# A decoder layer on one core: w_up too in Strassen products, 256 tokens wide, with sums of its blocks on GpSimd

## The chip, the cores and the metric

The kernel runs on one core of one Trainium2 chip. Its engines are TensorE (PE, matmuls and transposes), VectorE (DVE), ScalarE (ACT), GpSimd (POOL) and SyncE (SP, which only issues DMAs here). The metric is the device time of one execution in microseconds (us).

## What is computed

One hybrid decoder layer on 512 tokens of width 1024, all in float32:

```python
    hn = rms_norm(h, mix_pre_g)                     # w_in: q, k, v, u, gv
    ... MoBA attention beside chunked gMLP gating, both through w_o
    h = h + rms_norm(mixed @ w_o, mix_post_g)
    hn = rms_norm(h, mlp_pre_g)
    ff = square(relu(hn @ w_up))                    # (512, 1024) @ (1024, 4096)
    h = h + rms_norm(ff @ w_down, mlp_post_g)       # (512, 4096) @ (4096, 1024)
    gate = sigmoid(h @ w_ple_gate + b_ple_gate)
    h = h + rms_norm((p @ w_ple) * gate, ple_post_g)
```

The change is in the two products of the channel MLP, `w_up` and `w_down`, and in what stands around them.

## The kernel before

**Products in three matmuls.** Every float32 operand x is split in two parts of the faster type float32r: `x_hi` (ACT copies x, which rounds it) and `x_lo = x - x_hi` (DVE). A product is hi * hi + hi * lo + lo * hi, three matmuls into one PSUM bank (`product`, called on lines 1816 to 1821 of the profile). So each block of a weight or of activations costs one ACT and one DVE operation before PE may use it.

**The MLP in 8 steps.** A step is 512 of the 4096 hidden features. `up_tile(step, j)`, j from 0 to 3, makes 128 features by 512 tokens: 8 slices of the contraction by 3 matmuls, 24 matmuls of 512 columns. Its weights come as slabs of 128 x 512 through the buffer `raw` in SBUF, are multiplied by the gain `mlp_pre` in the split, and stay in a ring of 12 slots of `w_hi` and `w_lo`. ACT applies ReLU and square (`relu`, `f_square`) and leaves `f[step % 2]`, 4 tiles of 128 features by 512 tokens.

**w_down in Strassen products.** f and the step's 512 rows of `w_down` are each seen as 2 x 2 blocks (256 tokens by 256 features, 256 features by 512 columns). Seven products (`down_product(n)`, n = 7 * step + i, 12 matmuls of 512 columns) replace eight. Sums of f's blocks are made by DVE (`sum_e`, `sum_s2`, `sum_s3`, `sum_s4`). Sums of weight blocks are made by DMAs that add in SBUF, issued by POOL (`add_x`, `add_o`, lines 1674 and 1680), each behind the split of what the buffer held before. `t_split_hi` and `t_split_lo` split the weights (ring of 3), `a_split_hi` and `a_split_lo` the activations (ring of 4). `add_product` adds each filled product to `acc` in SBUF. PE's order for a step is product n, tile 0 of the next step, n+1, n+2, tile 1, n+3, tile 2, n+4, n+5, tile 3, n+6. The last step is done without Strassen, in 8 `down_tile`s of 12 matmuls.

**The order is written by hand.** Each engine has one queue, in program order: what waits at its head holds up all that is behind it. SP loads weights by its own list (`up_pair`, `x_raw`, `o_raw`), each entry behind the semaphore that frees its buffer.

**Around the MLP.** Before it, hn is turned by PE in 8 transposes (`turn_hn`), and ACT and DVE split the result from PSUM (`hn_turn_hi`, `hn_turn_lo`); `p @ w_ple` is computed and later spilled to DRAM (`ple_spill`), to make room for `acc`. After it, `add_mlp(t)` normalises `acc` and adds it to h, `turn_h2` transposes h, and `gate_tile` multiplies it by `w_ple_gate`. In the kernel before, h stays in SBUF all the time, and half of the gate's weights are split during the last steps.

Of the kernel before, what the change touches and what calls it, by code (L numbers as in the profile page):

```python
# [32 lines left out]
F32 = mybir.dt.float32  # L33
# [6 lines left out]
P = 128  # L40
# [29 lines left out]
SLAB_GATE = SLAB_UP + STEPS * KD  # L70
PAIRS_OF_SLABS = (SLAB_GATE + HALVES * KD) // 2
FIRST_PAIRS = KD // 2
UP_SLOTS = 12
# [15 lines left out]
T_RING, A_RING = 3, 4  # L89


def pair_in_stream(pair):

    first_up, first_gate = SLAB_UP // 2, SLAB_GATE // 2
    if pair < first_up:
        return pair
    if pair < first_gate:
        step, i = divmod(pair - first_up, KD // 2)
        return first_up + step // 2 * 16 + step % 2 * 4 + i
    return first_up + CHUNKS * 16 + pair - first_gate  # L100
# [31 lines left out]
def units_heads(unit):  # L132

    return [(s, pair, j) for s in range(2) for j, pair in enumerate(UNITS[unit][1])]

# [86 lines left out]
def hymba_layer(nc, x, xT, pT, weights, columns, rope, ws, rows, out):  # L222
# [6 lines left out]
    with ExitStack() as ctx:  # L229
# [44 lines left out]
        gain_post = place("gain_post", [P, D])  # L274
        at_work = top[0]
        work = place("work", [P, 2, W])
        at_junk = top[0]
# [27 lines left out]
        ple = place("ple", [P, TT, D], at=at_area)  # L305
# [10 lines left out]
        at_a = [at_area + 24 * KIB, at_area + 28 * KIB, at_area + 32 * KIB, at_junk]  # L316
# [3 lines left out]
        raw_x = [place(f"raw_x{i}", [P, 2, W], at=at_w_hi + 24 * KIB + 4 * KIB * i) for i in range(2)]  # L320
        raw_o = [place(f"raw_o{i}", [P, 2, W], at=at_w_lo + 24 * KIB + 4 * KIB * i) for i in range(2)]
# [79 lines left out]
        x_added, o_added = sem("x_added"), sem("o_added")  # L401
        t_hi_done, t_lo_done, a_hi_done, a_lo_done = (sem("t_hi_done"), sem("t_lo_done"),
# [14 lines left out]
        def ring(slab):  # L417
# [5 lines left out]
            i = slab - SLAB_GATE  # L423
            if i < KD:
                return (slab - SLAB_UP) % UP_SLOTS
            return UP_SLOTS + i - KD if i < KD + 4 else i - UP_SLOTS

        def gain_of(slab):
# [5 lines left out]
            if SLAB_UP <= slab < SLAB_GATE:  # L434
                return mlp_pre((slab - SLAB_UP) % KD)
# [8 lines left out]
        def raw_place(slab):  # L444
            if slab < KD:
                return first_raw[slab // 4][:, slab % 4, :]
            return raw[:, slab % 4, :]
# [22 lines left out]
        def last_weights(i):  # L470
# [4 lines left out]
            if i < 2:  # L475
                slot = (FIRST_LAST + i) % T_RING
                return source[:], t_hi[slot][:], t_lo[slot][:]
            return source[:], w_hi[:, 2 * i - 4:2 * i - 2, :], w_lo[:, 2 * i - 4:2 * i - 2, :]
# [1797 lines left out]
```

## Time and profile before

| | before |
|---|---|
| median of 3 runs (lowest to highest) | 599.71 us (599.58 to 599.74) |
| the profiled execution's own time | 599.75 us |
| its span in the profile | 598.0 us |
| PE, DVE, ACT, POOL busy | 99%, 65%, 52%, 14% |
| moved by DMA | 82.90 MB, 139 GB/s in the mean |

The span is what the hardware profiler recorded; the time of the execution is a little longer. Matmuls are pipelined: a matmul of 512 columns is drawn as 0.39 us long, and the next one starts before it ends. What counts is the distance from start to start.

### The profile page before, as it was taken

The page shows a single profiled execution, that of the slowest core. Times are in us where ns is not written, and L with a number is a line of the kernel's source. Part 1 is how long each engine was busy: PE and PEld are TensorE (multiplying, and loading weights), DVE is VectorE, ACT ScalarE, POOL GpSimd, SP SyncE. Part 2 cuts the span into 40 slices and gives each one's busy share as a digit, 9 for nine tenths or more (in the row PEclk, how much of TensorE's full clock was granted, in tenths as well). Part 3 has the DMA queues.
Part 4 walks back from the last instruction along what each step waited for, and adds up shares of the span by engine and source line. Part 5 has one row for each costly group of instructions (what it writes and reads, how often), then busy time and mean ns, then how long its engine had stood idle before and what let it go on. Part 6 is the DMA issues. An engine that isn't in the chain of part 4 may idle for free.

```text
span 598.0 us, 7772 instructions
## 1 busy us (share of the span) xinstructions
PE 589.8 (99%) x2920; PEld 491.2 (82%) x2920; DVE 389.1 (65%) x577; ACT 311.3 (52%) x541; POOL 82.4 (14%) x151
## 2 busy tenths in 40 slices
PE   9999999999999999999999999999999999999995
PEld 7888888888788888888888888888888888888885
DVE  5655544478765963956846938657667578569655
ACT  6845544666555745644634735545446355634422
POOL 0165333000101210001001001010010010001011
PEclk9999999999999999999999999999999999999999
DMA  8845332113101389646826647547377366234011
GB/s 274 311 152 176 114 105 71 67 41 99 42 2 36 107 231 312 181 154 126 252 63 159 210 106 154 198 88 195 141 147 223 87 149 224 85 134 184 0 72 71
DMA packets 24517, 82.90 MB, mean 139 GB/s; under 512 B 2848, under 2 KB 4256, under 8 KB 23968
## 3 DMA queue, kind: packets, MB, share of 16 engines
q1 hardware_dynamic: 18576, 59.78, 28.6%
q0 software_dynamic: 4032, 14.68, 14.5%
q10 hardware_dynamic: 1872, 7.95, 3.8%
q8 instruction: 23, 0.38, 0.2%
q14 instruction: 14, 0.11, 0.1%
HBM read 78.20 MB, written 4.19 MB: 138 GB/s over the span
## 4 chain that ended last, share of the span: by engine, by line
PE 97%; DVE 2%; ACT 0%; issue 0%; POOL 0%; DVEq 0%; ACTq 0%
PE psum L1816 30%; PE psum L1820 30%; PE psum L1821 30%; PE psum L1871 2%; PE psum L2003 1%; PE psum L1983 1%; PE psum L1925 1%; PE psum L1885 1%; DVE w_lo L508 0%; DVE stat L631 0%; PE psum L1908 0%; DVE h L1007 0%; PE psum L1933 0%; ACT probs L1218 0%; DVE h L713 0%
## 5 line engine op out<-in xcount | busy, mean ns | idle before, releaser
L508 DVE SCALAR_TENSOR_TENSOR w_lo<-raw,cols,w_hi 128x512 fp32r<-128x512 f32 x112 | 82.9, 784 | 43.7 <-ACT w_hi L1076 43.7
L1816 PE MATMUL psum<-actT_hi,w_hi 128*128 128x512 f32 x256 | 99.6, 389 | 0.0
L1820 PE MATMUL psum<-actT_lo,w_hi 128*128 128x512 f32 x256 | 99.6, 389 | 0.0
L1821 PE MATMUL psum<-actT_hi,w_lo 128*128 128x512 f32 x256 | 99.6, 389 | 0.0
L1076 ACT ACTIVATE w_hi<-raw,cols 128x512 fp32r<-128x512 f32 x112 | 74.2, 714 | 43.7 <-PE psum L1816 22.2
L1816 PE MATMUL psum<-w_hi,actT_hi 128*128 128x512 f32 (+1 forms) x230 | 89.5, 389 | 0.0
L1821 PE MATMUL psum<-w_hi,actT_lo 128*128 128x512 f32 (+1 forms) x230 | 88.0, 383 | 0.0
L1820 PE MATMUL psum<-w_lo,actT_hi 128*128 128x512 f32 (+1 forms) x230 | 87.8, 382 | 0.0
L1816 PE MATMUL psum<-t_hi,a_hi 128*128 128x512 f32 x212 | 82.6, 389 | 0.0
L1821 PE MATMUL psum<-t_hi,a_lo 128*128 128x512 f32 x212 | 82.5, 389 | 0.0
L1820 PE MATMUL psum<-t_lo,a_hi 128*128 128x512 f32 x212 | 82.5, 389 | 0.0
L837 DVE TENSOR_TENSOR t_lo<-raw_x,t_hi 128x1024 fp32r<-128x1024 f32 x28 | 34.2, 1223 | 52.7 <-ACT t_hi L1382 52.6
L1816 PEld LDWEIGHTS psum<-actT_hi,w_hi 128*128 128x128 f32 x256 | 48.1, 188 | 10.1
L1821 PEld LDWEIGHTS psum<-actT_hi,w_lo 128*128 128x128 f32 x256 | 48.0, 188 | 10.0
L1820 PEld LDWEIGHTS psum<-actT_lo,w_hi 128*128 128x128 f32 x256 | 48.0, 188 | 9.9
L1674 POOL DMA_DIRECT2D raw_x<-weights_dram x21 | 18.5, 883 | 258.2 <-DVE t_lo L837 258.2
L1821 PEld LDWEIGHTS psum<-w_hi,actT_lo 128*128 128x128 f32 x230 | 43.2, 188 | 8.5
L1816 PEld LDWEIGHTS psum<-w_hi,actT_hi 128*128 128x128 f32 x230 | 43.3, 188 | 8.2
L1820 PEld LDWEIGHTS psum<-w_lo,actT_hi 128*128 128x128 f32 x230 | 43.3, 188 | 8.0
L896 DVE TENSOR_TENSOR acc<-acc,psum 128x512 f32<-128x512 f32 x76 | 49.0, 682 | 1.1 <-PE psum L1821 1.1
L1821 PEld LDWEIGHTS psum<-t_hi,a_lo 128*128 128x128 f32 x212 | 39.8, 188 | 8.3
L1816 PEld LDWEIGHTS psum<-t_hi,a_hi 128*128 128x128 f32 x212 | 39.8, 188 | 8.3
(187 smaller groups left out, 903.9 us busy)
## 6 DMA issues: line engine op xcount, KB each, us to landing
raw<-weights_dram SPq DMA_DIRECT2D x66, 512.0 KB, 3.7
raw_o<-weights_dram SPq DMA_DIRECT2D x23, 512.0 KB, 3.5
raw_x<-weights_dram POOLq DMA_DIRECT2D x21, 512.0 KB, 5.5
raw_x<-weights_dram SPq DMA_DIRECT2D x9, 512.0 KB, 5.2
raw_o<-weights_dram POOLq DMA_DIRECT2D x7, 512.0 KB, 9.1
h<-x_dram ACTq DMA_DIRECT2D x4, 512.0 KB, 5.0
ple_spill<-ple ACTq DMA_DIRECT2D x1, 2048.0 KB, 10.1
out_dram<-h SPq DMA_DIRECT2D x7, 256.0 KB, 2.0
```

The lines of the kernel that those rows point to most:

```text
L508: nc.vector.scalar_tensor_tensor(out=w_lo[:, place_at, :], in0=source, scalar=gain, in1=high, op0=ALU.mult, op1=ALU.subtract).then_inc(sla ...
L837: nc.vector.tensor_tensor(t_lo[n % T_RING][:], t_source(n), t_hi[n % T_RING][:].bitcast(F32), ALU.subtract).then_inc(t_lo_done, 1)
L896: nc.vector.tensor_tensor(part, part, bank, how).then_inc(product_added, 1)
L1076: nc.scalar.activation(w_hi[:, place_at, :], source, ACT.Copy, scale=gain).then_inc(slab_hi, 1)
L1674: nc.gpsimd.dma_start(raw_x[step % 2][:], weights[down_in_stream(step, rows, half)], accum_op=ALU.add).then_inc(x_added, 16)
L1816: begin = nc.tensor.matmul(out, a_hi, b_hi, start=first, stop=False, skip_group_check=read_between)
L1820: nc.tensor.matmul(out, a_hi, b_lo, start=False, stop=False, skip_group_check=read_between)
L1821: return nc.tensor.matmul(out, a_lo, b_hi, start=False, stop=last, skip_group_check=read_between)
L1871: mm = nc.tensor.transpose(psum[:, banks[name], j * P:(j + 1) * P], source[:, j * P:(j + 1) * P], ident[:])
L1885: mm = nc.tensor.matmul(out, wsT[:, g, :], gv[:, :, g * GD:(g + 1) * GD], start=True, stop=True)
L1925: nc.tensor.matmul(psum[:, BANK_O, 0:P], warm[:], warm[:], start=True, stop=True)
L1983: mm = nc.tensor.transpose(psum[:, bank + s, k * P:(k + 1) * P], probs[:, place_in_group(unit), s, k * P:(k + 1) * P], ident[:])
```

## The change

`w_up` of steps 1 to 7 is computed in seven Strassen products as well. The 1024 rows of the contraction are two halves of 512, the step's 512 features two of 256, and the tokens two halves of 256. A product is 24 matmuls of 256 columns: 2 tiles of features by 4 slices of a contraction half by 3, with 256 tokens as the moving operand. Four sums of x blocks are made once (POOL, `sum_x`, split by ACT and DVE). Four sums of weight blocks are made per step by POOL (`sum_blocks`) in the raw buffers. Two PSUM banks hold the products; ACT copies partial results out (`copy_c`), and DVE adds or subtracts (`c_sum`), so that the four blocks C_11, C_22, C_12, C_21 of f appear one after the other. The gain `mlp_pre` is now applied to hn, not to the weights. Step 0 keeps full products.

For room, h is written to DRAM (`h_spill`) before the MLP and read again after it; `raw_x` and `raw_o` lie where h was. The gain of the MLP's norm is loaded late, and the ring of activations has 3 slots.

The diff, cut to its core:

```diff
+            def up_product(step, j):
+                bank = BANK_UP + (j in (BLOCK_21, BLOCK_T1, BLOCK_22))
+                pe.wait_ge(block_lo, q + 1)
...
+                for m in range(2):
+                    cut = slice(m * P, (m + 1) * P)
+                    for k in range(4):
+                        mm = product(up_bank(bank)[:, m, :], w_high[:, k, cut], w_low[:, k, cut],
+                                     x_high[:, k, :], x_low[:, k, :], begins and m == 0 and k == 0, k == 3,
+                                     read_between=True)
             for step in range(LAST):
                 n = PRODUCTS * step
-                down_product(n)
-                up_tile(step + 1, 0)
...
+                for j in range(PRODUCTS - 1):
+                    down_product(n + j)
+                    up_product(step + 1, j)
```

POOL, in the step loop and ahead of it:

```diff
+            def sum_blocks(step, target, block, n, split):
+                if split is not None:
+                    pool.wait_ge(block_lo, up_block(step, split) + 1)
+                nc.gpsimd.tensor_tensor(target, target, block, ALU.add).then_inc(block_summed, 1)
+                pool.wait_ge(block_summed, 4 * (step - 1) + n)
+            pool.wait_ge(x_lo_done, 2 * TT)
+            sum_x(SUM_E, x_part(xr, 1, 0), x_part(xr, 1, 1), ALU.subtract, 1)
...
                 add_x(step, 1, 1, 1)
                 if step:
                     add_o(step)
+                sum_blocks(up, first[:, :, left], first[:, :, right], 1, BLOCK_11)
+                sum_blocks(up, first[:, :, right], second[:, :, right], 2, None)
                 add_x(step, 1, 0, 2)
+                sum_blocks(up, first[:, :, left], second[:, :, right], 3, BLOCK_T1)
+                sum_blocks(up, first[:, :, left], second[:, :, left], 4, BLOCK_T2)
```

ACT, at the MLP's start:

```diff
             hn_turn_hi(6)
             hn_turn_hi(7)
+            for t in range(TT):
+                spill_h(t)
+            block_split_hi(0, 2)
+            block_split_hi(0, 3)
...
+            act.dma_start(ple_spill, ple[:]).then_inc(ple_spilled, 16)
             relu(0, 0)
             f_square(0, 0)
+            sum_split_hi(SUM_E)
+            t_split_hi(0)
             relu(0, 1)
+            block_split_hi(1, BLOCK_21)
+            block_split_hi(1, BLOCK_11)
             f_square(0, 1)
+            sum_split_hi(SUM_S2)
+            sum_split_hi(SUM_S3)
             a_split_hi(0)
```

DVE, at the start of a step:

```diff
+                if step:
+                    add_product(n - 1)
                 sum_e(step)
                 sum_s3(step)
-                if step:
-                    add_product(n - 1)
                 a_split_lo(n + 1)
                 sum_s2(step)
```

SP, at the MLP's start and at its end:

```diff
+            sp.wait_ge(h_spilled, 16 * TT)
             x_raw(0, 0, 0)
             o_raw(0, 0, 0, 1)
+            up_pairs(1, 1)
+            sp.wait_ge(block_lo, UP_SLOTS)
+            up_pairs(1, 0)
...
             sp.wait_ge(product_filled, 2 * FIRST_LAST)
+            sp.wait_ge(t_lo_done, FIRST_LAST + len(LAST_BLOCKS))
+            for t in range(TT):
+                sp.dma_start(h[:, t, :], h_spill[:, t, :]).then_inc(h_loaded[t], 16)
             sp.dma_start(ple_late[0][:], ple_spill[:, 0:2, :]).then_inc(ple_loaded[0], 16)
+            for pair in range(3, HALVES * KD // 2):
+                gate_pair(pair)
```

ACT and DVE, at the end:

```diff
+            last_t_hi(LAST_BLOCKS[2])
+            last_a_hi(LAST_TILES[2])
+            last_a_hi(LAST_TILES[3])
+            last_t_hi(LAST_BLOCKS[3])
+            gate_hi(2)
+            gate_hi(3)
             square_down(0)
...
+            last_t_lo(LAST_BLOCKS[3])
             add_product(FIRST_LAST - 1)
+            splits(SLAB_GATE + 4)
+            splits(SLAB_GATE + 6)
...
             tail_down(0)
```

The eight `down_tile`s of the last step are done in another order: tiles 0, 2, 3, 1 with features of the second half, then tiles 0 to 3 with those of the first, then the others whole.

## Rows read from the trace of the kernel before

**Rows 1.** The page: span, then busy us (share) xinstructions.

```profile
span 598.0 us, 7772 instructions
...
PE 589.8 (99%) x2920; PEld 491.2 (82%) x2920; DVE 389.1 (65%) x577; ACT 311.3 (52%) x541; POOL 82.4 (14%) x151
```

**Rows 2.** The page's chain that ended last: shares of the span.

```profile
PE 97%; DVE 2%; ACT 0%; issue 0%; POOL 0%; DVEq 0%; ACTq 0%
```

**Rows 3.** Timeline of PE: start us, length, engine, line, operation.

```profile
215.16 0.39 PE L1816 MATMUL psum<-actT_hi,w_hi 128*128 128x512 f32 x1
...
538.84 0.27 PE L1871 MATMUL psum<-ident,h 128*128 128x128 f32 x1
```

**Rows 4.** Busy us of each engine in one step, then clock, DMA share, GB/s.

```profile
294.80:335.60 40.80, 40.80 (x182) 33.78 (x181) 27.46 (x39) 20.31 (x31) 3.52 (x4) 1.00 0.59 155
```

**Rows 5.** Timeline of PE in the tail: 48 with 256 columns, first, last.

```profile
586.00 0.28 PE L1816 MATMUL psum<-w_hi,actT_hi 128*128 128x256 f32 x1
...
591.63 0.28 PE L1821 MATMUL psum<-w_hi,actT_lo 128*128 128x256 f32 x1
```

**Rows 6.** Groups of DVE and ACT, 254 to 498.8: busy us, mean ns, idle.

```profile
L896 DVE TENSOR_TENSOR acc<-acc,psum 128x512 f32<-128x512 f32 x70 | 45.1, 682 | 0.8 <-PE psum L1821 0.8
...
L837 DVE TENSOR_TENSOR t_lo<-raw_x,t_hi 128x1024 fp32r<-128x1024 f32 x24 | 29.4, 1223 | 51.3 <-ACT t_hi L1382 51.3
...
L843 DVE TENSOR_TENSOR a_lo<-f,a_hi 128x512 fp32r<-128x512 f32 x24 | 16.1, 688 | 0.4 <-ACT a_hi L1393 0.4
...
L508 DVE SCALAR_TENSOR_TENSOR w_lo<-raw,cols,w_hi 128x512 fp32r<-128x512 f32 x46 | 32.5, 749 | 12.5 <-ACT w_hi L1076 12.5
...
L1382 ACT ACTIVATE t_hi<-raw_x 128x1024 fp32r<-128x1024 f32 x25 | 26.3, 1054 | 26.2 <-DMA raw_x<-weights_dram 17.1 <-PE psum L1821 9.1
...
L1393 ACT ACTIVATE a_hi<-f 128x512 fp32r<-128x512 f32 x25 | 15.4, 618 | 0.0
```

**Rows 7.** Timeline of POOL and DVE, 29 to 58, where both work.

```profile
29.98 1.79 DVE L508 SCALAR_TENSOR_TENSOR w_lo<-raw,cols,w_hi 128x512 fp32r<-128x512 f32 x1
...
31.29 1.62 POOL L1604 TENSOR_TENSOR gv<-gv,ln_gb 128x512 f32<-128x512 f32 x1
...
39.57 1.29 POOL L1604 TENSOR_TENSOR gv<-gv,ln_gb 128x512 f32<-128x512 f32 x1
...
39.58 1.83 DVE L508 SCALAR_TENSOR_TENSOR w_lo<-raw,cols,w_hi 128x512 fp32r<-128x512 f32 x1
...
57.14 0.46 POOL L1629 TENSOR_TENSOR rope_tmp<-work,rope_sb 128x128 f32<-128x128 f32 x1 [3.44 <-ACT work L1157]
```

**Rows 8.** POOL's accumulating DMAs: groups by line, then landing us of raw_x.

```profile
L1674 POOL DMA_DIRECT2D raw_x<-weights_dram x21 | 18.5, 883 | 258.2 <-DVE t_lo L837 258.2
...
L1680 POOL DMA_DIRECT2D raw_o<-weights_dram x7 | 8.6, 1226 | 0.0
...
raw_x<-weights_dram POOLq DMA_DIRECT2D x21, 512.0 KB, 5.5
```

**Rows 9.** DMA: a window; the ACT queue; loads and spill to landing.

```profile
226.00:240.00 14.00, 14.00 (x63) 11.58 (x63) 4.96 (x7) 8.78 (x14) 0.87 (x1) 1.00 1.02 319
...
q10 hardware_dynamic: 1872, 7.95, 3.8%
...
raw<-weights_dram SPq DMA_DIRECT2D x66, 512.0 KB, 3.7
...
ple_spill<-ple ACTq DMA_DIRECT2D x1, 2048.0 KB, 10.1
```

**Rows 10.** Timeline at the MLP's start: hn's last splits, ple's last drains.

```profile
212.18 1.09 ACT L1098 ACTIVATE actT_hi<-psum 128x512 fp32r<-128x512 f32 x2 [1.14 <-PE psum L1871]
...
217.94 1.88 DVE L812 COPY ple<-psum 128x512 f32<-128x512 f32 x3
```

**Rows 11.** Timeline at the MLP's end: the first square_down and add_mlp.

```profile
528.88 1.06 ACT L1110 ACTIVATE junk_late<-acc 128x1024 f32<-128x1024 f32 x1 [4.43 <-DVE acc L1018]
...
532.79 1.22 DVE L962 TENSOR_TENSOR h<-h,acc 128x1024 f32<-128x1024 f32 x1
```

More of the change, by code:

```diff
@@ L69, with up_block @@
 LAST = STEPS - 1
-SLAB_GATE = SLAB_UP + STEPS * KD
-PAIRS_OF_SLABS = (SLAB_GATE + HALVES * KD) // 2
+SLAB_GATE = SLAB_UP
 FIRST_PAIRS = KD // 2
-UP_SLOTS = 12
+UP_SLOTS = 4
+BLOCK_21, BLOCK_11, BLOCK_T1, BLOCK_T2, BLOCK_T3, BLOCK_22, BLOCK_T4 = range(7)
+HALF_T = SEQ // 2
+SUM_E, SUM_S2, SUM_S3, SUM_S4 = range(4)
+def up_block(step, j):
+    return j if step == 0 else 4 + PRODUCTS * (step - 1) + j
 PRODUCTS = 7
@@ L88, with up_in_stream, gate_in_stream @@
 BEGINS_BANK = (True, True, False, False, False, False, False)
[L89 to L100, printed above, removed]
+T_RING, A_RING = 3, 3
+def up_in_stream(step, i):
+    return SLAB_UP // 2 + step // 2 * 16 + step % 2 * 4 + i
+def gate_in_stream(pair):
+    return SLAB_UP // 2 + CHUNKS * 16 + pair
 def down_in_stream(step, rows, half):
@@ L134, in units_heads, with in_last @@
     return [(s, pair, j) for s in range(2) for j, pair in enumerate(UNITS[unit][1])]
+def in_last(order, i):
+    return order.index(i)
+LAST_BLOCKS, LAST_TILES = (1, 3, 0, 2), (2, 3, 0, 1)
 def adds_until(n):
@@ L422, in ring @@
                 return KD + slab - SLAB_PLE
[L423 to L426, printed above, removed]
+            pair, second = divmod(slab - SLAB_GATE, 2)
+            return 2 * ((pair + 1) % UP_SLOTS if pair < UP_SLOTS else pair) + second
         def gain_of(slab):
@@ L483, in last_activations, with raw_of, block_source @@
             flat = lambda tile: tile[:].rearrange("p q n -> p (q n)")
-            return f[LAST % 2][:, k, :], flat(a_hi[slot]), flat(a_lo[slot])
+            if turn_a < A_RING:
+                slot = (FIRST_LAST + turn_a) % A_RING
+                return source, flat(a_hi[slot]), flat(a_lo[slot])
+            return source, last_a_hi_place[:], last_a_lo_place[:]
+        def raw_of(step):
+            return raw, (raw_second if step else raw_first)
+        def block_source(step, j):
+            first, second = raw_of(step)
+            left, right = slice(0, W // 2), slice(W // 2, W)
+            if step == 0:
+                return (second[:, :, left], first[:, :, left], second[:, :, right], first[:, :, right])[j]
+            return {BLOCK_21: second[:, :, left], BLOCK_22: second[:, :, right],
+                    BLOCK_T3: first[:, :, right]}.get(j, first[:, :, left])
@@ L486, in hymba_layer, with squared, hn_of @@
+        def squared(step, token_half, feature_half):
+            if step == 0:
+                return 2 * feature_half + 2
+            return 4 * step + {(0, 0): 1, (1, 1): 2, (0, 1): 3, (1, 0): 4}[token_half, feature_half]
+        C_11, C_22, C_12, C_21 = 1, 2, 3, 4
+        PLACE_OF_C = {C_11: (0, 0), C_22: (1, 1), C_12: (0, 1), C_21: (1, 0)}
+        def hn_of(i):
+            return i // 2, 1 - i % 2
         block = ctx.enter_context(nc.Block())
@@ L1387, in a_split_hi @@
                 if i in (0, 4, 5):
-                    act.wait_ge(f_done, 4 * step + (2 if i == 0 else 4))
+                    act.wait_ge(f_done, squared(step, *{0: (0, 0), 4: (0, 1), 5: (1, 1)}[i]))
                 else:
@@ L1685, in _ @@
             for step in range(LAST):
+                up = step + 1
+                first, second = raw_of(up)
+                left, right = slice(0, W // 2), slice(W // 2, W)
                 add_x(step, 1, 1, 1)
```

568 lines of the change are left out of this document (373 added, 195 removed).

## The prediction

> **What bounds the kernel now.** I read the busy shares first: TensorE (PE) is busy 99% of a 598.0 us span, VectorE (DVE) 65%, ScalarE (ACT) 52%, GpSimd (POOL) 14% [rows 1]. A busy share alone doesn't tell whether PE is fed, so next comes the chain of waits: 97% of it is PE [rows 2]. Then the stretch that the change touches. The channel MLP begins with the matmul at 215.16, and the first transpose of the new hidden state starts at 538.84 [rows 3]. Between lie 96 matmuls of step 0, 7 times 96 + 84, and 72 of the last step, 1428 in all: 323.68 / 1428 = 0.2267 us each, with PE busy all the time, so PE waits for nothing in the MLP. Only PE work can be saved there, and any new wait is paid in full. The window of one step says the same: PE 40.80 busy in 40.80 us, at full granted clock, DVE 27.46, ACT 20.31 [rows 4]. The profiled execution took 599.75 us (1.75 outside its span), the median of the runs is 599.71; the sum is made from 599.75.
>
> **Part 1: the matmuls.** Per step from 1 on, 96 up matmuls of 512 columns (21.76 us) become 7 products x 2 x 4 x 3 = 168 of 256 columns. A 256-column matmul starts every (591.63 - 586.00) / 47 = 0.1198 us [rows 5]: half the columns, more than half the time, since some 13 ns stay at either width (0.2267 - 0.1198 = 0.107 for 256 columns). So 168 x 0.120 = 20.16, and the gain is 1.60 us per step, 7 times: **-11.2 us**. The 84 matmuls of w_down's products, step 0 and the 72 of the last step keep their count. A step is 39.2 us at best.
> Here the Trainium skill says something else. TensorE: Matmul & The Clock Gate, section Back-to-back issue gap, gives a warm gap of N / 2.4 ns plus 2.5. By it the step would save 2.4 us and the sum be 5 us lower than mine; the measured pitches of both widths decide against it here.
>
> **Part 2: the steady steps.** Per step ACT gains 7 splits of 1024 elements and 3 copies for 8 splits of 512, DVE 7 splits of 1024 and 3 sums for 8 of 512. By the rows (1.22 for 1024, 0.68 for 512, some 0.07 less from start to start) DVE does 14 splits of 1024, 7 of 512, 4 + 3 sums and 12 additions: 14 x 1.15 + 26 x 0.61 = 32.0 of 39.2 us; ACT, likewise, 14 x 1.05 + 7 x 0.62 + 11 x 0.6 = 25.6 [rows 6]. Both fit. POOL is new: 4 sums of 1024 elements. 128 elements took 0.46 and 512 took 1.29, so 1024 come to 1.29 + 512 x 0.00216 = 2.4 us [rows 7]; with three accumulating DMAs at 0.88, 0.88 and 1.23 [rows 8] POOL has 12.6 us of work.
> What doesn't fit is the company of POOL and DVE. The split issued at 39.58 beside POOL's operation of 39.57 took 1.83 instead of 0.75 [rows 6]: it waited for POOL's 1.29 to end. At 29.98 and 31.29 they take turns, POOL's next one stretched to 1.62 by the DVE operation in front [rows 7]. So each POOL sum holds DVE operations with two SBUF operands for up to 2.4 us (the skill's SBUF - State Buffer, section Who interferes with whom, calls this an exclusive lock for the whole instruction, and lets additions with one operand in PSUM pass; the rows agree). Where does that meet PE? Take a step with time 0 at the end of up product T4, whose block C_21 is the last of f. ReLU and square on ACT end at 1.5; then DVE must make sum_e, sum_s3 and the low half of a(n+1) for the product that PE wants at 2.72 + 2.88 = 5.6. Unhindered this ends at 3.6. POOL's queue has add_x (behind t_lo of the second block, which I find at -1.4, since that waits for an accumulating DMA of 5.5 us), then add_o, then sum 1, from 0.7 to 3.1. DVE's sum_e follows to 3.7, POOL takes its turn with sum 2 to 6.1, then sum_s3 and a_lo end at 7.5: PE waits 1.9, in steps 1 to 6. Bounds: 0 (the sums fall into DVE's gaps or beside its additions) and 2.0. The rows show alternation both times two POOL operations followed each other, so I take 1.5, nearer the upper end: **+9.0 us**. Later deadlines in the step keep some 0.5 to 3 us.
>
> **Part 3: the start.** raw_x and raw_o now lie in h, so the SP queue waits for four spills of h before it loads anything for w_down, and behind those two loads stand the four of w_up for step 1. Turning hn now passes DVE, ACT, DVE; by the queue this ends at about 214.9, just before 215.16: 0 (at most 1 us). The spills are issued from 214.2 on, after ACT's last split of hn (before: 212.18 + 1.09, now behind two DVE operations) [rows 10]. The ACT queue moved 7.95 MB in 3.8% of the span, 350 GB/s [rows 9], so 2.1 MB are out after 6.0 us plus 1.6 to 2 of latency: 222.3. From there to the landing of w_up's last pair go 3.1 MB in the SP queue beside the ple spill of 2.1 MB, which is issued near 221 (its drains end a little later than 217.94 + 1.88 [rows 10]). At the 319 GB/s of 226 to 240, when the engines were full [rows 9], 5.24 MB take 16.4, so the landing is at 222.3 + 1.6 + 16.4 = 240.3. ACT waits for it in order: block 11 of step 1 stands ahead of f_square(0, 1), and behind it come two sums' high halves and a_hi(0). From landing to the first w_down product: 1.05 + 0.63 + 2 x 1.05 + 0.62 + 0.69 = 5.1, so 245.4. PE is ready for it at 215.16 + 96 x 0.2267 = 236.9. **+8.5 us**; bounds 1.5 (the load queue served before the spill: 3.1 MB at 319, landing 233.6) and 13 (accumulations in between, ReLUs 2 and 3 late for the next products).
>
> **Part 4: the end.** Let 0 be the end of the last w_down product (before: 522.52). The 72 matmuls run until 16.3 in either kernel (538.84), in a new order that needs C_21 later; its splits fit. But h must come back. SP waits for the last low half of the weights: behind 0 ACT has t_hi(0), two a_hi and t_hi(2), 3.3 to 4.4, and DVE ends t_lo(2) at 5.8. Then 4 loads of h (2.1 MB), half of ple (1.05 MB) and only then gate pair 3 (0.52 MB) are issued in one queue: 3.67 MB at 350 GB/s = 10.5 plus 1.6 = landed at 17.9. Both ACT's gate_hi(3) and DVE's split of the same pair stand ahead of square_down(0) and the tail's first additions. From the landing: two high halves 1.14, one low 0.65, two additions 1.2, square with its read 1.25, rstd 0.9, scaling and addition to h 2.5 (before: 528.88 to 534.0 with its wait) [rows 11]: 7.6, so h2 is ready at 25.5 and PE waits 9.2. **+9.2 us.** Bounds 7 (450 GB/s, above anything in rows 9) and 12 (270 GB/s). Later rows of the tail have 1 to 3 us of room.
>
> **The sum.** 599.75 - 11.2 + 9.0 + 8.5 + 9.2 = 615.3, say 615 us.
>
> **Rivals.**
> A (forecast): three stalls, all from work that stands in order behind something late: 615. Own range 608 to 625. Chance 0.47.
> B: the turns of POOL and DVE cost PE nothing, since sum 1 and sum 2 fall beside the PSUM additions; start and end as above: 606. For it: DVE has 7 us free per step. Against: sum_e can't start before POOL is in the middle of sum 1. 0.2.
> C: faster. The place is the transfers: if loads pass the ple spill and h's return isn't in front of gate pair 3's landing, because DMAs of one queue share the engines, the stalls at both ends shrink below the gain: 599.75 - 11.2 and 0 to 10 of rest is 588.5 to 598.5, most likely 594. It decides where pair 3 lands before 14 of part 4 (then the wait there is 5.3, and with 1.5 to 5 at the start the sum is under 599.7). For it: single loads of raw landed in 3.7 us [rows 9]. Against: 3.1 MB are ahead of it from 5.8 on, and ACT's order at the start needs all of w_up's pairs. 0.17.
> D: the loads share well at the start only: the tail waits 9.2, the start 1.5 to 5, the steps nothing: 599 to 603. 0.1.
> E: DVE becomes the bound: its 32.0 plus 4 x 2.4 of turns is 41.6 a step, with its own waits for the last sums 43.5, 7 x (43.5 - 40.8) + 8.5 + 9.2 more: 636. 0.06.
>
> **How the numbers follow.** Range 593 to 628: it leaves out the lower part of C and E, under 2 in 10 together. A measurement of this kernel tells 0.2% (1.2 us) from no change. Slower by more: A, B, E and some of D, 0.76. Within: 0.07, the rest of D and the upper edge of C. Faster: C, 0.17.
>
> **What would show it.** Up matmuls 0.120 apart with 256 columns (else part 1 is wrong); a step of about 40.7 us with a PE gap before the second w_down product, released by DVE's a_lo behind sum_e, and DVE splits of over 2 us beside POOL's sums (part 2); a gap of 8 us before the first w_down product, ACT idle until a load of raw ends (part 3); a gap of 9 us before the first transpose of h, ACT's split of a gate pair released by a DMA (part 4). A result under 599 would mean that the transfers of parts 3 and 4 came in time, over 628 that DVE bounds the steps.

## The result: 8% slower, and the profile after

The changed kernel takes 648.97 us (median of 4, 647.10 to 650.74), the one before beside it 599.73: a ratio of 1.0817 (95% interval 1.0782 to 1.0851). The forecast was 615, its range ended at 628. The profiled execution took 647.10 us with a span of 645.4, so 47.4 us more than the span of [rows 1].

The page of the kernel after, its busy time and the chain of waits; compare [rows 1, 2]:

```profile
span 645.4 us, 8965 instructions
...
PE 595.1 (92%) x3424; PEld 515.1 (80%) x3424; DVE 475.8 (74%) x595; ACT 337.2 (52%) x555; POOL 176.0 (27%) x187
...
PE 52%; DVE 30%; DMA 9%; issue 4%; ACT 3%; SPq 1%; POOL 0%; ACTq 0%; DVEq 0%; POOLq 0%
```

PE's share of the chain fell from 97% to 52%; DVE and DMAs now hold 39%. PE's timeline tells where (start, length, then in brackets the idle time in front and what ended it; compare [rows 3]). The pair at 378.76 and 379.96 are 10 pitches (distances from start to start) of the new up matmuls: 0.120 each.

```profile
246.98 0.77 PE L2081 MATMUL psum<-t_hi,a_hi 128*128 128x512 f32 x1 [9.44 <-issue]
...
338.44 0.47 PE L2081 MATMUL psum<-t_hi,a_hi 128*128 128x512 f32 x1 [2.94 <-DVE t_lo L966]
...
378.76 0.28 PE L2085 MATMUL psum<-actT_lo,up_hi 128*128 128x256 f32 x1
...
379.96 0.28 PE L2086 MATMUL psum<-actT_hi,up_lo 128*128 128x256 f32 x1
383.09 0.70 PE L2081 MATMUL psum<-t_hi,a_hi 128*128 128x512 f32 x1 [2.86 <-DVE t_lo L966]
...
584.48 1.94 PE L2136 MATMUL psum<-ident,h 128*128 128x128 f32 x8 [9.71 <-DVE h L1106]
```

The first and the last are the forecast waits of 9 us at the start and the end. The two in the middle weren't forecast: they stand ahead of product 0, the first of a step's seven w_down products (1.5 us in step 1, 2.6 to 2.9 in steps 2 to 6). The forecast wait, ahead of product 1, is there too, 2.37 us in step 0, 1.97 in step 1, and only 0.40 to 0.55 in steps 2 to 6. The windows of step 2, and of the 8 us behind the wait at its head (busy us of PE, PEld, DVE, ACT, POOL, then granted clock, DMA share, GB/s; compare [rows 4]):

```profile
338.44:383.09 44.65, 41.39 (x252) 37.15 (x253) 38.51 (x41) 23.83 (x32) 14.39 (x9) 0.96 0.54 142
...
338.44:346.40 7.96, 7.56 (x37) 6.44 (x38) 7.96 (x7) 1.26 (x2) 6.50 (x4) 0.79 0.72 133
```

A step takes 44.65 us, not 39.2; DVE is busy 38.5 of it, not the 32.0 of its durations alone; and behind the wait the granted clock is 0.79, so that 36 matmuls take 7.3 us where at full clock they take 5.6. The clock is as low behind the waits of 9.44 and 2.37 us in step 0 and at the heads of steps 3 to 6; each of these seven waits costs 1.5 to 1.7 us more than it shows. Behind the waits of 1.54 and 1.97 us in step 1 it stays at 1.00.

I cut the span at two places: the start of the first w_down product, and the end of the last one (its first matmul on PE's timeline plus 12 x 0.2267). Before: 236.9, then 285.6 for the seven steps, then 75.5 to the end of the span. After: 247.0, 311.3, 87.1. So the start lost 10.1 us, the end 11.6, and the steps 25.7, although their matmuls got 10 us shorter (a step without waits takes 39.34 us in the last experiments): 36 us of waits and lower clock.

How the head of step 3 comes to be late: SP's loads, POOL's issue of the accumulating DMA, and what waits for it.

```profile
365.68 1.23 SPq L1996 DMA_DIRECT2D raw_second<-weights_dram  x2
368.56 0.80 SPq L1996 DMA_DIRECT2D raw<-weights_dram  x2
369.69 0.33 SPq L2023 DMA_DIRECT2D raw_o<-weights_dram  x1
370.06 0.43 SPq L2014 DMA_DIRECT2D raw_x<-weights_dram  x1
...
371.95 0.89 POOL L1894 DMA_DIRECT2D raw_x<-weights_dram  x1 [10.31 <-DVE t_lo L966]
...
380.07 1.06 ACT L1572 ACTIVATE t_hi<-raw_x 128x1024 fp32r<-128x1024 f32 x1 [3.32 <-DMA raw_x<-weights_dram]
...
381.16 1.23 DVE L966 TENSOR_TENSOR t_lo<-raw_x,t_hi 128x1024 fp32r<-128x1024 f32 x1 [4.61 <-ACT t_hi L1572]
382.31 0.69 DVE L972 TENSOR_TENSOR a_lo<-f,a_hi 128x512 fp32r<-128x512 f32 x1
...
384.21 2.65 POOL L1911 TENSOR_TENSOR raw<-raw 128x1024 f32<-128x1024 f32 x1
...
385.24 2.19 DVE L990 TENSOR_TENSOR a_sum<-f 128x512 f32<-128x512 f32 x1
...
387.35 2.89 DVE L995 TENSOR_TENSOR f<-f 128x512 f32<-128x512 f32 x1
```

Six loads of 0.5 MB go out between 365.68 and 370.5, the accumulating DMA at 371.95 comes behind all of them and lands 8.1 us later, where [rows 8] had 5.5. It brings the weights of product 1. But on both engines the activations of product **0** are split behind them (a_lo at 382.31), so PE, ready at 380.1, starts product 0 at 383.09. From 384.21 POOL's sums then stretch DVE's two activation differences from 0.69 to 2.19 and 2.89; below this is called the lock. Over the whole kernel, median landing of the accumulating DMAs into raw_x and mean of POOL's sums 2 to 4 (ns):

```profile
raw_x<-weights_dram POOLq DMA_DIRECT2D x21, 512.0 KB, 7.0
...
L1911 POOL TENSOR_TENSOR raw<-raw,raw_second 128x1024 f32<-128x1024 f32 x21 | 60.5, 2881 | 30.1 <-DVE up_lo L832 29.5
```

Start and end, the two splits behind a late load:

```profile
241.36 1.06 ACT L1436 ACTIVATE up_hi<-raw 128x1024 fp32r<-128x1024 f32 x1 [8.62 <-DMA raw<-weights_dram]
...
576.29 1.15 ACT L1218 ACTIVATE w_hi<-gate_raw 128x512 fp32r<-128x512 f32 x2 [13.18 <-DMA gate_raw<-weights_dram]
```

### The profile page after: what moved, and what is told of

It is laid out like the page before. It is cut to its first block, busy times and chain, and to the rows that moved or that the text cites. A ratio compares the mean times of both kernels' runs of the same rounds, so it can differ in the third digit from the quotient of the medians.

```text
span 645.4 us, 8965 instructions
## 1 busy us (share of the span) xinstructions
PE 595.1 (92%) x3424; PEld 515.1 (80%) x3424; DVE 475.8 (74%) x595; ACT 337.2 (52%) x555; POOL 176.0 (27%) x187
## 4 chain that ended last, share of the span: by engine, by line
PE 52%; DVE 30%; DMA 9%; issue 4%; ACT 3%; SPq 1%; POOL 0%; ACTq 0%; DVEq 0%; POOLq 0%
PE psum L2081 16%; PE psum L2086 15%; PE psum L2085 15%; DMA raw_x<-weights_dram 7%; DVE t_lo L966 7%; DVE up_lo L832 5%; DVE a_lo L972 5%; DVE acc L1025 4%; DVE f L995 2%; PE psum L2136 2%; DVE a_sum L990 2%; DMA gate_raw<-weights_dram 2%; PE psum L2268 1%; DVE f L961 1%; PE psum L2248 1%
## 5 line engine op out<-in xcount | busy, mean ns | idle before, releaser
L1911 POOL TENSOR_TENSOR raw<-raw,raw_second 128x1024 f32<-128x1024 f32 x21 | 60.5, 2881 | 30.1 <-DVE up_lo L832 29.5
L2086 PE MATMUL psum<-sum_hi,up_lo 128*128 128x256 f32 x224 | 63.4, 283 | 0.0
L2085 PE MATMUL psum<-sum_lo,up_hi 128*128 128x256 f32 x224 | 63.4, 283 | 0.0
L2081 PE MATMUL psum<-sum_hi,up_hi 128*128 128x256 f32 x224 | 63.2, 282 | 0.0
L2085 PE MATMUL psum<-actT_lo,up_hi 128*128 128x256 f32 (+1 forms) x200 | 60.0, 300 | 0.0
L2086 PE MATMUL psum<-actT_hi,up_lo 128*128 128x256 f32 (+1 forms) x200 | 59.9, 300 | 0.0
L2081 PE MATMUL psum<-actT_hi,up_hi 128*128 128x256 f32 (+1 forms) x200 | 59.9, 299 | 0.0
L832 DVE TENSOR_TENSOR up_lo<-raw,up_hi 128x1024 fp32r<-128x1024 f32 x37 | 46.5, 1257 | 8.5 <-ACT up_hi L1436 8.5
L603 DVE SCALAR_TENSOR_TENSOR w_lo<-raw,cols,w_hi 128x512 fp32r<-128x512 f32 x48 | 37.7, 831 | 19.2 <-ACT w_hi L1220 19.1
L2086 PEld LDWEIGHTS psum<-t_hi,a_lo 128*128 128x128 f32 x216 | 43.2, 200 | 10.1
L2086 PEld LDWEIGHTS psum<-w_hi,actT_lo 128*128 128x128 f32 x230 | 43.2, 188 | 8.5
L2085 PEld LDWEIGHTS psum<-t_lo,a_hi 128*128 128x128 f32 x216 | 43.8, 203 | 7.6
```

What stands on the lines that cost most here:

```text
L603: nc.vector.scalar_tensor_tensor(out=w_lo[:, place_at, :], in0=source, scalar=gain, in1=high, op0=ALU.mult, op1=ALU.subtract).then_inc(sla ...
L832: nc.vector.tensor_tensor(up_lo[q % UP_SLOTS][:], block_source(step, j), up_hi[q % UP_SLOTS][:].bitcast(F32), ALU.subtract).then_inc(block ...
L1911: nc.gpsimd.tensor_tensor(target, target, block, ALU.add).then_inc(block_summed, 1)
L2081: begin = nc.tensor.matmul(out, a_hi, b_hi, start=first, stop=False, skip_group_check=read_between)
L2085: nc.tensor.matmul(out, a_hi, b_lo, start=False, stop=False, skip_group_check=read_between)
L2086: return nc.tensor.matmul(out, a_lo, b_hi, start=False, stop=last, skip_group_check=read_between)
```

## The experiments

All start from the kernel after, and all but the last are single executions, beside which the kernel before took 599.4 to 599.9. The four executions of the kernel after spread over 3.6 us, so a difference of 3 us between single ones shows little. One table of all, cut like the result (us). The time is the median where there are several; the three other columns are of the profiled execution and add up to its span (that execution took 647.1 for after and 594.6 for e11):

```
run            time     start   steps   end
before         599.7    236.9   285.6   75.5
after          649.0    247.0   311.3   87.1
e1a_a_first    652.0    247.2   316.5   86.7
e1b_t_late     632.1    247.3   294.8   88.3
e2_thin_sums   624.9    247.6   287.1   88.5
e3_start       642.0    238.3   312.5   89.5
e4_gate3       640.4    246.9   311.6   80.1
e5_hold        633.8    248.9   296.5   86.6
e6_adds_first  660.7    246.9   323.3   88.8
e7_all         622.9    237.3   307.1   76.7
e10_rest       616.3    237.4   300.6   76.5
e9_dve_sums    598.8    237.6   279.7   79.9
e8_rest_thin   598.0    237.6   279.0   79.6
e11_best       595.8    237.6   279.8   75.5
```

**Product 0's activations first.** On DVE, and in the same way on ACT:

```diff
                     block_split_lo(up + 1, BLOCK_21)
-                    t_split_lo(n + 8)
                     a_split_lo(n + 7)
+                    t_split_lo(n + 8)
                     block_split_lo(up + 1, BLOCK_11)
```

> One edit to the kernel after: at the end of each step ScalarE and VectorE split the activations of the next step's first w_down product ahead of the weights of its second, which wait for the accumulating DMA. Theory (order on the engines): the splits of product 1's weights, block 11's split, the adds, the two activation differences (stretched beside GpSimd's sums) and the a_lo split form one chain of about 12 us from the DMA's landing to product 1, and this chain isn't shortened. The gaps of 2.7 to 3.1 us ahead of product 0 of steps 2 to 6 vanish, but ahead of product 1 stand 3 to 4 us in place of 0.6 to 0.7, the period of a step stays at 43.5 to 44.6 us and the time at 641 to 649. Rival (head of line only): with product 0 freed nothing else is late, the period falls to 40 to 41.5 us and the time to 622 to 632. Rival (VectorE is the bound of the step, 44 us whatever the order): 44.6 us a step, 649, gaps moved about.

652.02 us, 3 over the first theory's band. The waits ahead of product 0 are gone, and ahead of product 1 stands this in step 3, 3.7 to 4.9 in steps 1 to 6:

```profile
392.43 0.77 PE L2081 MATMUL psum<-t_hi,a_hi 128*128 128x512 f32 x1 [3.97 <-issue]
```

Product 1 starts at 392.43, in the kernel after at 390.94: it hangs on the landing and the chain behind it, and the wait ahead of product 0 had hidden that. The first theory's chain is there, with waits up to 0.9 and periods (44.9 to 46.9) up to 2.3 us longer than it said; freeing the head of the line alone gains nothing. The small 0.4 to 0.55 ahead of product 1 in the kernel after was thus no sign that the lock is cheap.

**Product 1's weights split later still**, behind the activation differences; POOL's sums, which wait for that split, then begin later:

```diff
                     a_split_lo(n + 7)
                     block_split_lo(up + 1, BLOCK_11)
...
                 sum_s3(step)
+                if step:
+                    t_split_lo(n + 1)
                 a_split_lo(n + 1)
```

> As the run with the activations first, and the split of product 1's weights is moved further back, behind block 11's split and the two activation differences of the next step; GpSimd, which waits for that split before its next DMA and the sums behind it, so begins its sums about 3 to 4 us later. Theory (order on the engines): both gaps go, the one ahead of product 0 (2.7 to 3.1 us, with 1.7 us of lower clock behind it) and the one ahead of product 1 (0.6 to 2.1); the period of a step is 39.2 to 40.5 us, 24 to 30 us less in all, 618 to 625. Rival (VectorE bound by the lock): GpSimd's sums stretch other VectorE work as much, the period stays above 43 us and the time above 638. Rival (the DMA is simply late): product 2's weights are late next by about the 3 us by which their DMA is issued later; 41.5 to 43 us a step, 630 to 640.

632.12 us, 41.9 us a step: between the theories, with the time that the last rival gives. The waits moved on to product 2 (1.59) and product 3:

```profile
387.56 0.50 PE L2082 MATMUL psum<-t_hi,a_hi 128*128 128x512 f32 x1 [1.59 <-DVE t_lo L966]
```

That rival's reason is only part of it. ACT's t_hi, which waited for the DMA, ended at 385.34, but DVE began product 2's t_lo at 386.29, behind an a_lo of 2.74 and a sum_s4 of 2.89 us, both beside POOL's sums. So DVE came last, by some 1.0 us; without the lock some 0.6 of the 1.59 would have stayed for the DMA (an estimate from these times). The lock had moved with the sums. The 1.6 us waits left the clock at 1.00.

**The lock taken away.** POOL's sums cover 8 of each 256 columns and leave the others unsummed, so what the kernel computes is incomplete; every wait stays:

```diff
-                nc.gpsimd.tensor_tensor(target, target, block, ALU.add).then_inc(block_summed, 1)
+                nc.gpsimd.tensor_tensor(target[:, :, 0:8], target[:, :, 0:8], block[:, :, 0:8], ALU.add
+                                        ).then_inc(block_summed, 1)
```

> GpSimd's four sums of w_up's blocks per step cover only 8 of each 256 columns, so the other columns are left unsummed; all waits stay. Each sum falls from 2.7 us to well under 0.5, and with it VectorE's stretched operations (2.2, 2.9 and 2.8 us) to their 0.69. Theory (the accumulating DMA's landing, 8 us after its issue, gates product 0): the gap ahead of product 0 stays at 2 to 3 us in steps 2 to 6 with its lower clock; the gap ahead of product 1 (0.6; 2.1 in step 1; 2.5 at the start) goes; the period is 43 to 44 us and the time 635 to 641. Rival (the lock is what costs, as the forecast had it): all the gaps of the steps go, 39.2 to 40.5 us a step, 614 to 622.

624.90 us, 24 less, and again between the two. As the first theory says, the wait ahead of product 1 is gone and one ahead of product 0, ended by t_lo, stays; but it is 0.6 to 2.0 us, not 2 to 3, and the clock is at 1.00 behind it:

```profile
332.81:373.65 40.84, 39.59 (x252) 35.96 (x253) 32.44 (x41) 24.05 (x32) 5.42 (x9) 1.00 0.59 155
```

DVE is busy 32.4 us, which is the forecast's sum of durations. I had underrated the lock: 24 of the steps' 36 us of loss go with it. It and the late landing add up to waits behind which the clock falls. The two aren't cleanly apart in this run, though: the accumulating DMA ahead of a step's head landed in 6.3 to 7.7 us here, against 7.3 to 8.2 in the kernel after.

**The DMA's landing:** SP holds back its two loads of w_down's blocks (1 MB) that aren't urgent.

```diff
                     up_pairs(step + 2, 0)
+                    sp.wait_ge(x_added, 16 * (3 * (step + 1) + 1))
                     o_raw(step + 1, 1, 1, 0)
```

> One edit: at the end of each step SyncE holds back its two loads of w_down's blocks that aren't urgent (1 MB) until the accumulating DMA has landed on which product 1 of the next step waits. Theory (bunching: with w_up the step's loads go out within 6 us, right ahead of this DMA, at 315 GB/s, where before they were spread): it lands in 5 to 6 us instead of 8.1, the gap ahead of product 0 falls from 3 to under 1 us, so that the clock stays, and the period goes from 44.6 to 41 to 42.5 us: 629 to 639. Rival (such a DMA takes 7 to 8 us beside GpSimd's and VectorE's work, whatever else loads): landing, gaps and period as after, 645 to 651.

633.77 us: the theory holds, and 14.8 us of the steps' loss go. Around the head of step 3 (SP, POOL, ACT, PE), and the landing over the kernel:

```profile
374.26 0.33 SPq L2023 DMA_DIRECT2D raw_o<-weights_dram  x1
...
368.83 0.89 POOL L1894 DMA_DIRECT2D raw_x<-weights_dram  x1 [10.30 <-DVE t_lo L966]
...
374.27 1.06 ACT L1572 ACTIVATE t_hi<-raw_x 128x1024 fp32r<-128x1024 f32 x1 [0.59 <-DMA raw_x<-weights_dram]
...
385.14 0.47 PE L2082 MATMUL psum<-t_hi,a_hi 128*128 128x512 f32 x1 [2.01 <-issue]
...
raw_x<-weights_dram POOLq DMA_DIRECT2D x21, 512.0 KB, 5.2
```

With the loads away it lands after 5.4 us, product 0 has no wait over 0.3, and what is left is 1.7 to 2.0 us ahead of product 1 in steps 1 to 6: the forecast's own scene, with the 1.9 us that it had worked out (behind two of them, 1.99 and 1.98, the clock falls, and the period is 43.2 instead of 41.6). So the forecast's picture of a step is that of a kernel whose DMA comes in 5.5 us; the change's own loads took that away. The steps are still 21 us over what their matmuls need.

**Where the sums stand.** The activations first, and POOL's third DMA ahead of its first two sums:

```diff
+                add_x(step, 1, 0, 2)
                 sum_blocks(up, first[:, :, left], first[:, :, right], 1, BLOCK_11)
                 sum_blocks(up, first[:, :, right], second[:, :, right], 2, None)
-                add_x(step, 1, 0, 2)
```

> Two edits: ScalarE and VectorE split the activations of the next step's first product ahead of the weights of its second (alone that gave 652), and GpSimd issues its third accumulating DMA of a step before its first two sums and not behind them, so the sums begin some 8 to 10 us later and don't stretch VectorE's activation differences. Theory (the lock counts by where it falls: on the chain from the DMA to product 1): both gaps at the head of a step go, little else is late, 39.3 to 41 us a step, 619 to 629. Rival (the lock costs VectorE's queue the same wherever the sums stand): the wait moves to products 2 or 3 and block T1's product, 42 us a step or more, 633 or more.

660.65 us, the slowest of all: the rival, and dearer than it said. Waits at block T1's product and the w_down product behind it, 45 to 48 us a step:

```profile
357.63 0.39 PE L2081 MATMUL psum<-sum_hi,up_hi 128*128 128x256 f32 x1 [2.62 <-DVE up_lo L832]
...
362.56 0.47 PE L2081 MATMUL psum<-t_hi,a_hi 128*128 128x512 f32 x1 [1.81 <-DVE acc L1025]
```

**Start and end.** At the start the split of block 11, whose weights land last, goes behind the preparation of products 0 and 1, on ACT (and in the same way on DVE):

```diff
             block_split_hi(1, BLOCK_21)
-            block_split_hi(1, BLOCK_11)
             f_square(0, 1)
...
                 a_split_hi(n + 1)
+                if step == 0:
+                    t_split_hi(1)
+                    block_split_hi(1, BLOCK_11)
```

> One edit at the start: the split of block 11 of step 1, whose weights land at 241, is put behind the preparation of the first two w_down products on ScalarE and VectorE. Theory (head of line behind a late load): the 9.4 us ahead of the first w_down product go to under 1, the 1.5 us of lower clock behind it too; product 1 then needs its weights, whose accumulating DMA was issued at 230, at about 245.7, and comes 0 to 3 us late. 8 to 12 us less, 637 to 641. Rival (bandwidth at the start: the other loads are as late): product 1 or block 11's product waits for 5 us or more, and under 5 us are gained, 644 to 649.

642.02 us, 1 us short of the expected band. The first w_down product begins 8.7 us sooner, with 0.31 in front:

```profile
238.26 0.47 PE L2083 MATMUL psum<-t_hi,a_hi 128*128 128x512 f32 x1 [0.31 <-issue]
```

The mechanism is shown; 1.2 us of it went in the steps and 2.4 at the end, whose waits grew. At the end, gate pair 3's load goes ahead of h's return:

```diff
             gate_pair(2)
+            gate_pair(3)
...
-            for pair in range(3, HALVES * KD // 2):
+            for pair in range(4, HALVES * KD // 2):
```

> One edit at the end of the kernel after: SyncE issues the load of gate pair 3, whose buffer has been free since pair 0's split, before it waits for the last w_down product and reads h back, not behind those reads. Theory (head of line: ScalarE and VectorE hold pair 3's splits ahead of the first token tile's square, and wait 13 us for this load): the wait of 9.7 us ahead of the turns of h goes to 0 to 1.5, with the 1.7 us of lower clock behind it; 8.5 to 11.5 us less, 638 to 640.5. Rival (the read of h itself is late): the wait stays above 5 us, ended by the load of h, and the time is 644 to 649.

640.39 us, 8.6 less than the median of the kernel after; the end itself is 7.0 shorter, a little under the 8.5 to 11.5 expected. The first turns of h wait for nothing; the next load of a gate pair is in the way next, and h's second tile waits 2.54:

```profile
583.85 0.87 PE L2137 MATMUL psum<-ident,h 128*128 128x128 f32 x6 [2.54 <-DVE h L1106]
```

**All repairs with the sums moved.** e7 has both of these, the held loads, the activations first, e6's order on POOL, and product 0's weights split ahead of a wait for block 22:

```diff
-                c_sum(up, C_22)
                 if up < LAST:
                     t_split_lo(n + 7)
-                else:
+                c_sum(up, C_22)
+                if up == LAST:
                     last_t_lo(LAST_BLOCKS[0])
```

> All repairs together: the start's split of block 11 behind the first two products' preparation, gate pair 3's load early, the two loads held back until the accumulating DMA has landed, the first product's activations split first, GpSimd's sums behind its third DMA, and the split of product 0's weights ahead of the wait for block 22's product, so that the DMA behind it goes out about 2 us sooner. Theory (the matmuls give 11 us, and all that was lost are waits, which these edits take): the steps 39.2 to 40 us, the start's 14 us down to 0 to 3, the end's 12 to 1 to 3: 590 to 600, at or a little under the kernel before. Rival (one engine is short of time in the steps and the gaps only move): 41.5 us a step or more, 606 or more.

622.85 us: the rival. Start and end came out (237.3 and 76.7), the steps did not, 48.5 us for step 0 and 42.6 to 44.3 from then on, with e6's waits at block T1's product and behind it. This order doesn't take the lock away, nor does the other one tried (e10).

**The same repairs in POOL's old order; then with the sums thin; then with the sums on DVE.** e10 is e7 without e6's edit, e8 adds the thin sums to e10. e9 takes the four sums off POOL and gives them to DVE:

```diff
                 sum_s4(step)
+                sum_blocks(up, 1)
                 t_split_lo(n + 2)
+                sum_blocks(up, 2)
                 block_split_lo(up, BLOCK_T1)
                 add_product(n + 1)
+                sum_blocks(up, 3)
...
                 a_split_lo(n + 4)
+                sum_blocks(up, 4)
```

> The same repairs with GpSimd's sums whole and where the change has them. Theory (the lock falls on the two activation differences ahead of product 1): no gap ahead of product 0, 2 to 2.2 us ahead of product 1 as in the run with the held loads alone, 41 to 42 us a step, 613 to 620, and 20 to 24 us over the run with thin sums. Rival (the lock costs only what the late DMA left uncovered): 40 us a step or less, under 605.

> The repairs of start, end, the held loads, the first product's activations split first and the earlier split of product 0's weights, with GpSimd's sums in their old order but only over 8 of each 256 columns (the other columns are left unsummed). Theory (what the repairs leave is the port's lock alone): the heads of the steps have no gap above 0.5 us, 39.2 to 39.8 us a step, 590 to 598, the matmuls' 11 us less the 3 to 5 us left at start and end. Rival (VectorE's and ScalarE's order is short even without the lock, as the 1.2 to 2.1 us gaps with thin sums alone suggest): 40.5 us a step or more, 601 or more.

> The same repairs, and the four sums of a step are taken whole by VectorE (1.2 us each, 4.9 us a step) in place of GpSimd (2.7 to 3.3 us each, beside which VectorE is stretched by about 8 us a step). Theory: VectorE's busy time in a step falls from 38.5 to 34 to 36 us, under the 39.2 us of the matmuls; 39.3 to 40.3 us a step, gaps under 1 us, 591 to 603: as fast as the kernel before or faster. Rival (VectorE's queue is too full at the head of the step, whoever locks it): 41 us a step or more, 606 or more.

616.27, 597.98 and 598.83 us: all three times in the theory's bands, e8 at the top of its own. e10 lies 18.3 us over e8, a little under the 20 to 24 expected; from step 1 on two of its steps take 41.8 us, the other four 43.2 to 44.0, with waits of up to 3.6 or a lower clock. A step's window in e10, e8 and e9, a fence each:

```profile
411.21:452.97 41.76, 39.59 (x255) 35.96 (x253) 39.18 (x41) 23.84 (x32) 14.38 (x9) 1.00 0.58 144
```

```profile
319.92:359.25 39.33, 39.33 (x254) 35.89 (x253) 32.57 (x41) 24.07 (x32) 5.82 (x9) 1.00 0.61 161
```

```profile
320.32:359.66 39.34, 39.34 (x254) 35.90 (x253) 36.38 (x45) 23.95 (x32) 3.52 (x5) 1.00 0.62 161
...
L1021 DVE TENSOR_TENSOR raw<-raw,raw_second 128x1024 f32<-128x1024 f32 x20 | 24.3, 1216 | 0.0
...
L995 DVE TENSOR_TENSOR f<-f 128x512 f32<-128x512 f32 x6 | 4.1, 684 | 0.0
```

The reader is to see DVE's third number: 39.18 with the sums on POOL, 32.57 with thin sums, 36.38 with DVE making all four sums itself. POOL's help cost DVE 6.6 us a step where the work itself costs it 3.8. And in e9's step PE is busy 39.34 of 39.34. Between e10 and e8 the lock costs the steps 21.6 us, 3.1 a step; the times lie only 18.3 apart because e8's end is 3.1 longer: there the second tile of h waits 2.28 us, in e10 0.42.

**The last:** e9, with gate pair 4's load early as well and, at the start, product 1's weights split ahead of the last square. The load, against the kernel after:

```diff
+            gate_pair(3)
             sp.dma_start(gain_post[:], rows["mlp_post"]).then_inc(post_loaded, 16)
+            gate_pair(4)
             sp.wait_ge(product_filled, 2 * FIRST_LAST)
```

> The repairs with the sums on VectorE, and two more: product 1's weights are split again ahead of the last square at the start, so that the next accumulating DMA goes out some 3 us sooner (in the run with VectorE's sums product 2 waits 1.9 us for it), and gate pair 4's load, too, goes ahead of the reads of h (there ScalarE waits 8.2 us for it, and the turns of h's second tile 2.6 us). Theory: the wait ahead of product 2 falls under 0.5, the one ahead of the second turns from 2.6 to under 1 with its lower clock of some 1 us behind it, the steps stay at 39.3: 593 to 596, ratio 0.989 to 0.994 to the kernel before. Rival (the second tile waits for the read of h or the squares anyway): 597 to 599, no faster than before by more than 0.4%.

595.83 us (5 executions, 594.63 to 596.03) against 599.71, a ratio of 0.9935 (0.9921 to 0.9949): 0.65% faster than the kernel before, with the interval clear of no change, and inside the expected band. The end is back at 75.5. The wait ahead of product 2 is down only to 0.89, one of 0.76 stands ahead of product 1, and one of 1.70 ahead of product 3; all three are in step 0, and from then on none between two matmuls of 256 or 512 columns is over 0.3 us:

```profile
PE 580.8 (98%) x3424; PEld 506.7 (85%) x3424; DVE 460.5 (78%) x623; ACT 338.3 (57%) x555; POOL 100.7 (17%) x159
...
PE 88%; DVE 6%; ACT 2%; DMA 2%; issue 1%; ACTq 0%; POOL 0%; DVEq 0%; POOLq 0%
...
244.05 0.47 PE L2091 MATMUL psum<-t_hi,a_hi 128*128 128x512 f32 x1 [0.76 <-issue]
...
250.82 0.50 PE L2091 MATMUL psum<-t_hi,a_hi 128*128 128x512 f32 x1 [0.89 <-DVE t_lo L966]
...
258.45 0.47 PE L2091 MATMUL psum<-t_hi,a_hi 128*128 128x512 f32 x1 [1.70 <-DVE acc L1035]
```

## Why the prediction was wrong

The direction and three of its four parts held; the time was 32 us too low (647.1 for the profiled execution against 615.3), of which part 2 holds 27. The step that failed is part 2's scene of a step's head: it put the weights of product 1 in time, so it had no wait ahead of product 0, and it had no lower clock behind any wait.

**Part 1, right.** The pitch is 0.120 as measured before, and a step without waits takes 39.34 us in e9 and e11, against 40.80: 10.2 us over seven steps, for 11.2 in the sum. The rule that the forecast took from the Trainium skill's page TensorE: Matmul & The Clock Gate, section Back-to-back issue gap, would have given nearly 17. The page gives it for an isolated matmul; the measured pitches of this stream, 0.2267 and 0.120, don't bear it out.

**Part 2, the step that failed.** The sum put +9.0 here; measured are 35.9. Three of its points went wrong, and one held.

- "Behind t_lo of the second block, which I find at -1.4, since that waits for an accumulating DMA of 5.5 us": the 5.5 of [rows 8] was taken over as if it were a property of the DMA. At the head of step 3 it took 8.1, and t_lo ended at +2.3 on that clock (381.16 + 1.23 against T4's end at 380.1). e5 brings its end back to -0.7 (375.36 + 1.23 against product 0's start at 377.29) with nothing but 1 MB of loads held for some 8 us. The change itself moved w_up's loads into that place. The transfer was costed by its median before, not in the company that the new order of loads gives it; mending that alone gives back 14.8 of the 35.9 us.
- "Later deadlines in the step keep some 0.5 to 3 us": the one with the least room was product 0's, whose a_lo stands behind that t_lo in both queues. It took 16.3 us of waits in six steps, against 7.8 ahead of product 1 (step 0 included). These are gaps between matmuls less the pitch.
- The clock was left out. Behind the two waits in step 0 and those at the heads of steps 2 to 6 it cost 1.5 to 1.7 us each time, 11.3 in all. The three come to 35.4; half a us stays spread over the steps.
- "PE waits 1.9" of the lock, with bounds of 0 and 2.0: right for its scene (1.7 to 2.0 in e5), and 1.5 a step was too low a choice. The whole lock was dearer than its first wait: 3.1 a step between e10 and e8, since waits of over 2 us and a lower clock came with it. The kernel after doesn't show the scene itself: its small waits ahead of product 1 in steps 2 to 6 are what the larger ones ahead of product 0 left over, as e1a shows. The Trainium skill's SBUF - State Buffer, section Who interferes with whom, has it as an exclusive lock between VectorE and GpSimd; the runs agree: 0.69 became 2.17 to 3.62 beside POOL's sums in the kernel after, and was back at 0.69 when POOL made none. The forecast also said that its rows agree on additions with one operand in PSUM; they hold no such case. The trace of the kernel after does, a DVE addition that lies wholly within a POOL sum and isn't stretched:

```profile
351.54 2.66 POOL L1911 TENSOR_TENSOR raw<-raw,raw_second 128x1024 f32<-128x1024 f32 x1
...
352.57 0.68 DVE L961 TENSOR_TENSOR f<-f,psum 128x512 f32<-128x512 f32 x1
```

**Part 3, right.** Forecast +8.5, with w_up landed at 240.3 and the first product at 245.4; measured +10.1, 241.3 and 247.0. e3 shows the cause, the place of block 11's split. What was missed is the lower clock behind it, 1.5 us, which falls in the steps and is counted above.

**Part 4, right.** Forecast 9.2, measured a wait of 9.71, with gate pair 3's weights split 18.0 us behind the last product where the forecast had 17.9, and an end 11.6 us longer, the rest by lower clock and h's later tiles. e4 shows the cause for 7 of them, e11 the next load of the same kind for the remainder.

**The rivals.** E had the nearest time, 636, by DVE as the bound at 43.5 us a step. The period was 44.6, but E isn't what happened: DVE had 6 us free in each step, and e5 and e10 brought the period of some steps to 41.5 to 41.8 with DVE as busy (38.5 and 39.2). Order, arrival and the lock ahead of PE's products bound it, not DVE's load. C asked for all transfers in time, which is about what e10 has, and that took 616; under 600 came only with the sums off POOL as well (e9, e11).

What stays open is why the clock fell behind some waits and not behind others: not their length alone, since it fell behind one of 1.74 us in e8 and not behind one of 3.60 in e10 (below). How much of the steps' loss belongs to the late landing and how much to the lock isn't shown either: removing the one gave 14.8 us, removing the other 24.2, together more than the 35.9 that there were. Step 0 still takes 43.5 us in e11, 4.1 more than the others; its three waits make up 3.8.

## What to carry to other kernels

When an edit adds loads, write the new order of DMA issues down beside the deadlines, and cost each transfer that something waits for in that company; a median landing holds for the old order only. When a wait is removed, look at the next product's chain from the same arrival before you count the gain. Work given to an idle GpSimd wasn't free for VectorE here, where VectorE was reading SBUF with two operands: if VectorE does the work in less time than it would be held up, leave it there.

## What the runs showed of the hardware

- The granted clock fell behind PE waits as short as 1.7 us, though not behind each of them. Behind the 2.94 us wait at the head of step 2 it was 0.79 over the next 8 us, behind e5's 1.99 us wait at 300.35 it was 0.78 over 7.65 us, behind e1b's waits of 1.6 us it stayed at 1.00. In the kernel after one such fall cost 1.5 to 1.7 us. The shortest wait with a fall behind it (e8, product 2 of step 0) and the longest between matmuls without one (e10, product 1 of step 1), each with the window behind it:

```profile
250.76 0.50 PE L2086 MATMUL psum<-t_hi,a_hi 128*128 128x512 f32 x1 [1.74 <-DVE t_lo L966]
...
250.76:258.70 7.94, 7.94 (x39) 6.92 (x40) 7.79 (x10) 5.67 (x9) 1.69 (x3) 0.79 0.60 132
```

```profile
290.08 0.47 PE L2085 MATMUL psum<-t_hi,a_hi 128*128 128x512 f32 x1 [3.60 <-issue]
...
290.08:298.00 7.92, 7.92 (x46) 7.04 (x47) 7.92 (x11) 5.36 (x8) 3.32 (x2) 1.00 0.22 32
```

- GpSimd's additions of 1024 f32 elements per partition took 2.64 to 3.27 us in the kernel after, VectorE's 1.22 in e9.
- A VectorE operation of 0.69 us with both operands in SBUF took 2.17 to 3.62 beside such a sum in the kernel after; one with an operand in PSUM kept its 0.68 (352.57 in the kernel after).
- An accumulating DMA of 0.5 MB issued behind six loads of as much, all within 6 us, took 8.1 us; with two of the six held back 5.4.
